# First microseconds of a two-layer trunk kernel: the second token tile loaded, squared and normed in another order

## The reference

```python
def rmsnorm(x, g):
    xf = x.astype(jnp.float32)
    y = xf * lax.rsqrt(jnp.mean(xf * xf, axis=-1, keepdims=True) + EPS)
    return (y * g.astype(jnp.float32)).astype(x.dtype)

    for l in range(DEPTH):
        xn = rmsnorm(x, pre_mix_g[l])
        proj = xn @ w_in[l]
        u_lru, g_lru, q, k, v, gate_a, gate_b = slices of proj
        y_a = rglru_branch(u_lru, g_lru, ...) @ w_pa[l]      # width-4 convolution, two gates, a scan
        y_b = swa_sink_attention(q, k, v, cos, sin, ...) @ w_pb[l]   # rotary angles from positions
        mixed = (gate_a * y_a + gate_b * y_b) @ w_o[l]
        x = x + rmsnorm(mixed, post_mix_g[l])
        ...                                                  # and a feed-forward part
```

## Time and profile before

| what | value |
|---|---|
| median of three runs | 806.5 us |
| profiled execution, span | 806.89 us, 805.1 us |
| TensorE matmul busy | 793.7 us, 99% |
| VectorE busy | 602.4 us, 75% |
| ScalarE busy | 460.2 us, 57% |
| GpSimd busy | 75.3 us, 9% |
| loads | 156.48 MB, mean 194 GB/s |

### The profile page before, as it was taken

One profiled execution on the slowest core, in us unless ns is written; L12 is line 12 of the kernel. 1 busy time (PEld: TensorE's weight loads), 2 busy tenths in 40 slices (PEclk: granted clock), 3 DMA queues, 4 the chain that ended last, 5 costly groups with the idle time before them and its releaser, 6 DMA issues.

```text
span 805.1 us, 10534 instructions
## 1 busy us (share of the span) xinstructions
PE 793.7 (99%) x4250; PEld 667.3 (83%) x4250; DVE 602.4 (75%) x602; ACT 460.2 (57%) x591; POOL 75.3 (9%) x135
## 2 busy tenths in 40 slices
PE   7999999999999999999999999999999999999997
PEld 5897898888888888888889889988888888888885
DVE  6799897647689878667489869965567896985762
ACT  5567976633456555535455788865436555465341
POOL 3840000000120000000011100000003100000000
PEclk9999999999999999999999999999999999999999
DMA  9776444455387786962476745434654869769601
GB/s 293 260 244 199 147 147 155 138 176 209 109 309 228 221 310 182 260 212 104 157 223 223 260 129 185 158 106 156 222 195 146 279 179 293 213 225 261 209 0 53
DMA packets 84276, 156.48 MB, mean 194 GB/s; under 512 B 7314, under 2 KB 27906, under 8 KB 84228
## 3 DMA queue, kind: packets, MB, share of 16 engines
q1 hardware_dynamic: 80000, 147.42, 54.1%
q0 software_dynamic: 4224, 8.39, 6.2%
q10 hardware_dynamic: 4, 0.00, 0.0%
HBM read 154.75 MB, written 1.05 MB: 194 GB/s over the span
## 4 chain that ended last, share of the span: by engine, by line
PE 88%; DVE 4%; POOL 3%; issue 2%; DMA 2%; ACT 1%; DVEq 0%; POOLq 0%; ACTq 0%
PE work L771 13%; PE work L773 13%; PE work L772 13%; PE acc L771 8%; PE acc L773 8%; PE acc L772 8%; PE work L857 3%; PE work L858 3%; PE work L859 3%; PE work L763 3%; PE work L764 3%; PE work L765 3%; POOL turned_by L640 1%; DMA lru_a<-in_w_ffn_gate 1%; DVE weights_lo L1534 1%
## 5 line engine op out<-in xcount | busy, mean ns | idle before, releaser
L1534 DVE TENSOR_TENSOR weights_lo<-weights_raw,weights_hi 128x2048 fp32r<-128x2048 f32 x114 | 261.0, 2295 | 87.9 <-ACT weights_hi L1147 87.4
L1147 ACT ACTIVATE weights_hi<-weights_raw 128x2048 fp32r<-128x2048 f32 x116 | 221.7, 1916 | 160.8 <-PE work L773 84.8
L771 PE MATMUL work<-weights_hi,act_a_hi 128*128 128x512 f32 x416 | 164.3, 395 | 0.0
L773 PE MATMUL work<-weights_hi,act_a_lo 128*128 128x512 f32 x416 | 162.3, 390 | 0.0
L772 PE MATMUL work<-weights_lo,act_a_hi 128*128 128x512 f32 x416 | 161.9, 389 | 0.0
L771 PE MATMUL acc<-weights_hi,act_b_hi 128*128 128x512 f32 x240 | 94.7, 395 | 0.0
L773 PE MATMUL acc<-weights_hi,act_b_lo 128*128 128x512 f32 x240 | 93.6, 390 | 0.0
L772 PE MATMUL acc<-weights_lo,act_b_hi 128*128 128x512 f32 x240 | 93.4, 389 | 0.0
L771 PEld LDWEIGHTS work<-weights_hi,act_a_hi 128*128 128x128 f32 x416 | 78.1, 188 | 16.8 <-issue 0.8
L773 PEld LDWEIGHTS work<-weights_hi,act_a_lo 128*128 128x128 f32 x416 | 78.1, 188 | 16.6
L772 PEld LDWEIGHTS work<-weights_lo,act_a_hi 128*128 128x128 f32 x416 | 78.2, 188 | 15.5
(11 more groups left out here) (216 smaller groups left out, 1258.9 us busy)
## 6 DMA issues: line engine op xcount, KB each, us to landing
weights_raw<-in_w_in SPq DMA_DIRECT2D x43, 1024.0 KB, 5.2
weights_raw<-in_w_ffn_gate SPq DMA_DIRECT2D x16, 1024.0 KB, 7.6
weights_raw<-in_w_ffn_up SPq DMA_DIRECT2D x12, 1024.0 KB, 5.3
weights_raw<-in_w_ffn_down SPq DMA_DIRECT2D x12, 1024.0 KB, 4.9
weights_raw<-in_w_pa SPq DMA_DIRECT2D x8, 1024.0 KB, 5.0
weights_raw<-in_w_pb SPq DMA_DIRECT2D x8, 1024.0 KB, 5.0
weights_raw<-in_w_o SPq DMA_DIRECT2D x8, 1024.0 KB, 5.0
q_feat<-in_w_ffn_down SPq DMA_DIRECT2D x6, 1024.0 KB, 9.3
```

Of the source, the lines that this page charges most:

```text
L771: mm(dst, xh, wh, start=first, stop=False)
L773: return mm(dst, xl, wh, start=False, stop=final)
L1147: activate(w_hi[:, SLOT[n], :], raw_slot(RAWS[n]), ACT.Copy).then_inc(hi_done.sem, 1)
L1534: v.tensor_tensor(w_lo[:, SLOT[n], :], raw_slot(RAWS[n]), bits(w_hi[:, SLOT[n], :]), ALU.subtract).then_inc(split_done.sem, 1)
```

## The change

Six edits, all ahead of the first layer or in its first products. The load of token tile 1 is issued ahead of the second half of panel kv 0. The load of panel q0 0 and of the positions is issued ahead of the loads of the small vectors. ScalarE squares tile 1 right after the first half of kv 0, ahead of the copy of tile 0's first four blocks, and makes the second half of kv 0 between the two copies of tile 0. VectorE norms tile 1 in two halves, and makes the low part of tile 0's second four blocks after that. TensorE's second group of unread transposes is gone. The products of the kv panels by tile 0 are made in passes of two matmuls, in an order of their own, each pass with a wait for only what it reads.

```diff
-WARM = (5, 8)
+WARM = 5
@@ SyncE
             first_half(0, 0).then_inc(head_loaded, 16)
+            sp.dma_start(xres[:, 1, :], x[0, P:S, :]).then_inc(x_loaded[1], 16)
             first_half(0, 1).then_inc(raw_loaded[0].sem, 16)
-            sp.dma_start(xres[:, 1, :], x[0, P:S, :]).then_inc(x_loaded[1], 16)
             load(0, 1)
+            load(0, 2)
+            sp.dma_start(pos_i[:, :], positions.rearrange("a (t p) -> p (a t)", p=P),
+                         allow_slow_non_contiguous=True).then_inc(pos_loaded, 16)
 ...
-            load(0, 2)
-            sp.dma_start(pos_i[:, :], positions.rearrange("a (t p) -> p (a t)", p=P),
-                         allow_slow_non_contiguous=True).then_inc(pos_loaded, 16)
@@ TensorE
-            keep_busy(WARM[0])
 ...
-            keep_busy(WARM[1])
+            def turn_first(t):
+                for h in range(2):
+                    dst = claim(0, "xn", 2 * t + h)
+                    if h == 0:
+                        pe.wait_ge(head_normed, t + 1)
+                    else:
+                        pe.wait_ge(*xs_done.at(0, t + 1))
+                    for k in range(4):
+                        f = (4 * h + k) * P
+                        ins = nc.tensor.transpose(dst[:, k * P:k * P + P], QTOK[:, t, f:f + P], ident[:, :])
+                    ins.then_inc(turned.sem, 1)
+
+            keep_busy(WARM)
+            turn_first(0)
@@ first_products
+                    pe.wait_ge(head_hi, 1)
+                    pe.wait_ge(*xa_hi_done.at(l, 1))
+                    passed(0, 0, w_hi, xn_hi)
+                    pe.wait_ge(*head_split.at(l, 1))
+                    passed(0, 0, w_lo, xn_hi)
+                    pe.wait_ge(*xa_done.at(l, 1))
+                    passed(0, 0, w_hi, xn_lo)
+                    pe.wait_ge(*hi_done.at(l, 1))
+                    passed(0, 1, w_hi, xn_hi)
+                    passed(0, 1, w_hi, xn_lo)
+                    split_ready(AT["kv", 0])
+                    passed(0, 1, w_lo, xn_hi)
+                    turn_first(1)
+                    pe.wait_ge(head_hi, 2)
+                    pe.wait_ge(*xa_hi_done.at(l, 2))
+                    passed(1, 0, w_hi, xn_hi)
+                    pe.wait_ge(*xa_done.at(l, 2))
+                    passed(1, 0, w_hi, xn_lo)
+                    pe.wait_ge(*head_split.at(l, 2))
+                    passed(1, 0, w_lo, xn_hi)
+                    pe.wait_ge(*hi_done.at(l, 2))
+                    passed(1, 1, w_hi, xn_hi)
+                    passed(1, 1, w_hi, xn_lo)
+                    split_ready(AT["kv", 1])
+                    passed(1, 1, w_lo, xn_hi).then_inc(tile0.sem, 1)
                     for j in range(2):
-                        pe.wait_ge(*head_split.at(l, j + 1))
 ...
-                    pe.wait_ge(*xa_done.at(l, 4))
-                    for j in range(2):
+                        pe.wait_ge(*xa_done.at(l, 3 + j))
                         t_panel_product("kv", j, acc[:, 2, :], xn_hi, xn_lo, 1).then_inc(panel_used.sem, 1)
@@ ScalarE
             half_hi(0, 0).then_inc(head_hi, 1)
+            act.wait_ge(x_loaded[1], 16)
+            mean_square(1, xres[:, 1, :], ms_done.sem, 2)
+            xa_hi(0, 0, "xn", 0, range(1))
             act.wait_ge(*raw_loaded[0].at(0, LOADED[0]))
             half_hi(0, 1).then_inc(hi_done.sem, 1)
-            xa_hi(0, 0, "xn", 0)
-            act.wait_ge(x_loaded[1], 16)
-            mean_square(1, xres[:, 1, :], ms_done.sem, 2)
+            xa_hi(0, 0, "xn", 0, range(1, 2))
@@ VectorE
             half_lo(0, 0).then_inc(head_split.sem, 1)
-            xa_lo(0, 0, "xn", 0)
+            xa_lo(0, 0, "xn", 0, range(1))
             dve.wait_ge(*hi_done.at(0, 1))
             half_lo(0, 1).then_inc(split_done.sem, 1)
-            dve.wait_ge(rstd_done.sem, 2)
-            v.scalar_tensor_tensor(QTOK[:, 1, :], xres[:, 1, :], rstd[:, 1:2],
-                                   acc[:, 2:4, :].rearrange("p b f -> p (b f)"),
-                                   ALU.mult, ALU.mult).then_inc(xs_done.sem, 1)
+            normed_first(1)
+            xa_lo(0, 0, "xn", 0, range(1, 2))
             dve.wait_ge(head_hi, 2)
```

More of the change, by code:

```diff
@@ L734, in keep_busy @@
                     nc.tensor.transpose(work[3][:, 0:P], ident[:, :], ident[:, :])
-            keep_busy(WARM[0])
-            for h in range(2):
-                dst = claim(0, "xn", h)
-                if h == 0:
-                    pe.wait_ge(head_normed, 1)
-                else:
-                    pe.wait_ge(*xs_done.at(0, 1))
-                for k in range(4):
-                    f = (4 * h + k) * P
-                    ins = nc.tensor.transpose(dst[:, k * P:k * P + P], QTOK[:, 0, f:f + P], ident[:, :])
-                ins.then_inc(turned.sem, 1)
-            keep_busy(WARM[1])
+            def turn_first(t):
[11 more added lines that the diff above has]
+            turn_first(0)
             def layer(l, first, last_layer):
@@ L984, in first_products, with passed @@
-                    ins.then_inc(tile0.sem, 1)
-                    pe.wait_ge(*xa_done.at(l, 4))
-                    for j in range(2):
+                    def passed(j, half, weights, acts):
+                        wp = t_panel(weights, SLOT[AT["kv", j]], 4)
+                        for k in range(2 * half, 2 * half + 2):
+                            last = mm(acc[:, 0, :], acts[:, 4 * j + k, 0:P], wp[:, k, :],
+                                      start=(j, k) == (0, 0) and weights is w_hi and acts is xn_hi,
+                                      stop=(j, k) == (1, 3) and weights is w_lo)
+                        return last
@@ L1153, in mean_square, with xa_hi @@
                                    accum_out=mean_sq[:, n:n + 1]), sem, value)
-            def xa_hi(l, first, name, t):
-                for h in range(2):
+            def xa_hi(l, first, name, t, halves=range(2)):
+                for h in halves:
                     m = first + 2 * t + h + 1
```

18 lines of the change are left out of this document (7 added, 11 removed).

## The result

| | before | after |
|---|---|---|
| median of 22 runs each, us | 806.59 (806.36 to 807.15) | 807.60 (806.73 to 809.7) |
| profiled execution, span | 806.89, 805.1 | 807.07, 805.3 |
| TensorE busy, matmuls | 793.7 us, 4250 | 792.9 us, 4242 |

The ratio is 1.0014, with an interval of 1.0008 to 1.0020: the kernel after is slower by 1.0 us. That lies within 0.2% of no change, but on the other side of it than forecast, and above the range. The same source run once more as e1 gave 807.42 against 806.56, ratio 1.0012 [1.0003, 1.0021]. The profiled execution of after is one of its quick ones, 807.07, and that of before took 806.89: the two profiles are 0.18 apart where the medians are 1.0 apart.

What follows compares the result with a forecast made beforehand. Bounding line: VectorE's head, GpSimd's angle chain, VectorE from 43.15, TensorE from 52.07 to the end. Minus 0.45 at 43.15, carried to the end, gave 806.44 for a profiled run and 806.05 for the median; range 805.0 to 807.2.

Steps and rivals of the forecast that it cites:

- TensorE's head: TensorE's first products: first pass at 9.48 instead of 10.86, kv 0 by tile 1 at about 16.9 against 18.23, 1.3 us early.
- fourth rival: Without the unread transposes TensorE's clock stays low in the head: 806.9, or about 810 if for all 24 products; chance 0.08.
- VectorE's head: VectorE's first norms and splits up to `pos_float`: nearly full, no work removed, so it and the angle chain are 0.3 us early.
- the sum on its line: On the bounding line: minus 0.45 at 43.15, the same at 52.07, 59.30 and 60.47; 806.05 for the median.
- The splits from panel 4 on stay where they are: VectorE's later panel splits: loads are paced by a queue moving the same bytes, so these splits do not move.
- The eight unread transposes are inside that difference and not on top of it.: TensorE's head: the removed transposes' 1.61 us are already counted in the 1.3 us by which TensorE is early.
- From there TensorE's own work to the end: Last part of the bounding line: from 52.07 on, TensorE's own work was taken to bound the kernel to the end.
- TensorE's 1.3 us become a wait at 52.07 of 0.85: At the first gate products: TensorE's 1.3 us from the head turn into a wait of 0.85 for VectorE's `conv`.

Runs made afterwards that it cites:

- e3: Kernel before with only its second eight unread transposes taken out: 808.0 us, +1.44, ratio 1.0016.
- e4: Kernel before with `pos_float` moved ahead of the low part of tile 1: 806.75 us, +0.19.
- e10: Kernel after with the second eight unread transposes back and the small vectors' loads ahead of panel 2's again: 806.52 us, -0.17.
- e12: Kernel after with only the small vectors' loads back ahead of panel 2's: 807.42 us, +0.73.
- e2: Kernel after with the second eight unread transposes put back behind the turning of tile 0: 806.4 us, -0.16.
- e13: Kernel after with eight transposes just before the first layer's first gate products, none back in the head: 806.85 us against 806.87, -0.02.
- e5: Kernel before with three quarters of GpSimd's accumulating load, which runs beside the gate panel's load, left out: 806.2 us, -0.47.
- e6: Kernel after with three quarters of GpSimd's accumulating load, which runs beside the gate panel's load, left out: 806.33 us, -0.34.
- e7: Kernel after with the second eight unread transposes back and three quarters of GpSimd's accumulating load beside the gate panel's load left out: 806.15 us, -0.52.
- e8: Kernel after with three unread transposes back behind the turning of tile 0: 807.68 us, +1.01.
- e15: Kernel after with eight transposes before the first gate products of the second layer: 807.92 us, +1.05.
- e11: e10 with ten more transposes where TensorE waits for the first gates: 806.01 us, -0.68.
- e16: Kernel after with eight transposes back in the head and ten more before the first layer's first gate products: 806.07 us, -0.80.

## Why the prediction was wrong

- **TensorE's head.** Right: 16.9 forecast, 16.84 measured, where the pace rises in time. A part of the close fit is luck: the first pass came at 9.72 and not 9.48, although the turning ahead of it came 0.29 sooner than in the earlier trace rows. The fourth rival's slow products came in e1 and e3. It gave 0.65 at the end of the head (18.9: e1 has 18.90) and 806.9. What was left of it at q1 was 0.27, close to the 0.35 worked out.
- **VectorE's head and the sum on its line.** 0.3 forecast at `pos_float`, 0.49 measured, of which 0.21 is the new order and 0.28 the earlier start of VectorE's first norm; over the profiles the stretch from that norm to `pos_float` goes from 10.2 to 11.3 us in kernels with this order, and has 10.8 in before. -0.45 forecast at the first q1 product, -0.49 measured, and that agreement is luck: only 0.24 comes by the angles, and 0.25 from the step at 53.57 that was long in before. The way was another too: the chain is done before the pair of splits, and VectorE's own splits bind at 42.9.
- **"The splits from panel 4 on stay where they are"** failed in this profile: 38.50 against 37.86. With the pair at 37.86 VectorE would have gone on near 42.5, as e4 with its pair at 37.97 did at 42.38, and not at 42.91. Which edit moves the splits is open: 37.5 to 38.9 in the three kernels with the vectors' loads ahead again (e10 to e12).
- **"The eight unread transposes are inside that difference and not on top of it."** This is the step that failed. As time on TensorE it holds. But with sixteen instructions less ahead of it the gate panel's load lands 0.7 later, at a place without slack, and a packet of the instruction queue then falls into its flight. In numbers: off alone +1.44 (e3), back in the head -0.16 (e2), back elsewhere -0.02 (e13), and none of it when the load cannot bind (e5 and e6, 0.13 apart). By e1 and e2 the removal costs 1.0, by e3 1.4. The sum gave it 0. Forecast and measurement are 1.5 apart (-0.45 and +1.0): the other edits brought about -0.2, and this one cost 1.0 to 1.4. By e5 to e7 even the -0.2 is not shown.
- **"From there TensorE's own work to the end"** was the gap that let this pass. The trace of before had the wait of 0.81 at 663.70; the sum ended at 60.47 and left it out.
- **"TensorE's 1.3 us become a wait at 52.07 of 0.85", at no cost.** 1.04 in the profile, harmless there, as 0.79 to 1.56 were in e2, e6, e8, e12 and e15. After the waits of 1.95 and 1.96 in e7 and e10 the clock read 0.59 and the first q1 product was 1.4 to 2.1 late. This widens the spread upwards; the median owes it little.

Shown are the effect of the instructions ahead of the load (e2, e13 and e8, e15), that it works through this load (e6), and the split of the landings by the packet's place. That the packet itself holds the load back is inferred. Its size is for it, 0.9 us of one engine against a landing 0.7 later; against it, it is 16 KB beside 2 MB, and no run could move it without its instructions. Open is also whether the wait at the gates is to blame for the three executions above 809: none of the 33 executions of e11, e13 and e16, which fill that wait, had a mean clock under 0.998, against 7 of 110 in after and its other variants. That is few, and two executions of e15 took 809.2 at 0.998.

The best kernels are e11 and e16: 806.01 and 806.07, each with ratio 0.9993 [0.9984, 1.0002] to before. Either interval alone still holds 1; two kernels that agree make a gain of 0.7 us likely.

## What to carry to other kernels

Follow the bounding line past the place of the edit, to the last wait of the span, and ask of each wait behind it what it hangs on: a gain ends at the first place without slack whose releaser did not move. Removing idle work is an edit of its own, to be tried apart from the rest: unread instructions can be holding a clock, filling a wait, or only counting. Where a change of a few instructions far away moves a load's landing, compare where the instruction queue's packets fall in both traces.

## What the runs showed of the hardware

- One 16 KB packet of the instruction queue comes for 250 TensorE instructions (34 for 8500). A 1 MB load issued ahead of it, beside a block sum on another queue, landed in 10.0 to 10.7 us (18 loads), one issued behind it in 9.5 to 9.9 (10 loads). The packet takes 0.9 us of one DMA engine.
- A wait of 1.95 us ahead of the gates was followed by a granted clock of 0.59 over 54 to 58, in the middle of dense products. The Trainium skill, "TensorE: Matmul & The Clock Gate", section "HAM oscillation — how this bites in real kernels", tells of idle gaps within a kernel after which products run at the low clock again. The traces of e7 and e10 agree in kind, with gaps shorter than the page's example has; after waits of 0.2 to 1.56 us in seven other profiles the clock stayed at 1.00.
- TensorE's spacing of 512-column products was 0.43 us at the low clock and 0.23 at the full one. Without the second eight transposes the first twelve went at the low one in two profiles (e1, e3) and all or nearly all at the full one in six.
- A GpSimd operation on 64 columns takes 0.37 us between VectorE's splits, and 2.1 to 2.5 where it meets one. In the kernel after the last twelve operations of the chain all start between 33.1 and 38.1, in the stretch without a split, and the chain's end moves by 4.7 us for 0.5 at its start and a pair of splits that comes 0.64 later:

```profile
30.96 2.11 POOL L641 TENSOR_TENSOR angle<-angle,turned_by 128x64 f32<-128x64 f32 x1
33.16 0.37 POOL L640 TENSOR_SCALAR turned_by<-turns 128x64 f32<-128x64 f32 x1
```

The Trainium skill, "SBUF — State Buffer", section "Who interferes with whom", says that VectorE and GpSimd share a pair of ports as an exclusive lock. The rows agree, with sixfold durations under a split.
